# Sample states read and updated through four tiles of the array side by side, heads h and h+2 paired in partition halves

## The reference

```python
# q, logf, k: (B, L, H, 128); v: (B, L, H, 128); s0: (B, H, 128, 128); per block of tokens:
A = jnp.cumsum(lfc, axis=1)
inter = jnp.einsum('bthk,bhkv->bthv', qc * jnp.exp(A), S)
...
scores = jnp.einsum('bthk,bshk,btshk->bths', qc, kc, decay)
intra = jnp.einsum('bths,bshv->bthv', scores, vc)
AL = A[:, -1]
S_new = (jnp.exp(AL)[..., None] * S
         + jnp.einsum('bshk,bshv->bhkv', kc * jnp.exp(AL[:, None] - A), vc))
...
# then: o = rmsnorm per head * gnorm_w * silu(g); x += concat(conv, o) @ w_out; x += moe(rmsnorm(x))
```

## Time and profile before

| what | value |
|---|---|
| median of 3 runs | 1188.64 us (1186.55 to 1191.05) |
| the profiled execution, its own time | 1185.52 us |
| its span, first to last instruction | 1183.6 us |
| mean granted clock of PE | 0.985 of full speed |
| busy: PE, PEld, DVE, ACT, POOL | 95%, 40%, 35%, 14%, 3% |
| DMA, mean over the span | 365 GB/s |

### The profile page before, as it was taken

The page is one execution under the profiler, slowest core; times in us unless marked ns, Lnnn a source line. Parts: engine busy times, 40 slices in busy tenths (PEclk is TensorE's granted clock), DMA queues, the critical chain, the costliest instruction groups (busy, mean ns, idle before and its releaser), DMA issues.

```text
span 1183.6 us, 14962 instructions
## 1 busy us (share of the span) xinstructions
PE 1125.0 (95%) x5841; PEld 468.7 (40%) x5841; DVE 410.0 (35%) x702; ACT 167.7 (14%) x287; POOL 36.2 (3%) x55
## 2 busy tenths in 40 slices
PE   6999999899999999999999999999999999999994
PEld 5787864433333333333333333333333333333331
DVE  2144184643333333333333333333333333333333
ACT  3100112511111111111111111111111111111112
POOL 0000121110000000000000000000000000000000
PEclk9999999889999999999999999999999999999996
DMA  9962126569999999999999999999999999999991
GB/s 303 334 192 84 72 80 207 190 250 412 428 426 428 430 427 429 428 427 430 427 429 429 427 431 427 427 430 427 427 430 427 427 430 429 427 430 427 427 429 58
DMA packets 47375, 432.05 MB, mean 365 GB/s; under 512 B 3824, under 2 KB 18740, under 8 KB 22774
## 3 DMA queue, kind: packets, MB, share of 16 engines
q1 hardware_dynamic: 45792, 428.14, 87.6%
q0 software_dynamic: 752, 2.77, 0.8%
q10 hardware_dynamic: 805, 0.82, 0.2%
HBM read 428.00 MB, written 3.71 MB: 365 GB/s over the span
## 4 chain that ended last, share of the span: by engine, by line
PE 65%; DMA 30%; ACT 2%; DVE 2%; issue 1%; SPq 0%; ACTq 0%; DVEq 0%
PE ps L1153 36%; DMA ring<-in_w_up 15%; DMA ring<-in_w_gate 14%; PE ps L939 9%; PE ps L1109 4%; PE ps L1136 4%; PE ps L1041 3%; PE ps L1144 2%; PE ps L1192 1%; PE ps L958 1%; PE ps L927 1%; ACT R L521 1%; DMA x<-in_x_sample 1%; PE ps L1022 1%; PE ps L1119 1%
## 5 line engine op out<-in xcount | busy, mean ns | idle before, releaser
L1153 PE MATMUL ps<-ring,R 128*64 128x512 f32 x3072 | 694.1, 596 | 15.4 <-DMA ring<-in_w_up 10.4
L1153 PEld LDWEIGHTS ps<-ring,R 128*64 128x64 f32 x3072 | 210.2, 137 | 415.9 <-issue 368.4
L816 DVE SCALAR_TENSOR_TENSOR x<-ps,gates,x 128x1024 f32<-128x1024 f32 (+1 forms) x96 | 123.0, 1281 | 131.4 <-PE ps L1136 131.4
L939 PE MATMUL ps<-R,ring 128*128 128x320 f32 x384 | 112.1, 443 | 1.2 <-DVE R L579 1.2
L823 DVE TENSOR_TENSOR R<-ps,R 128x512 f32<-128x512 f32 x32 | 22.1, 692 | 240.5 <-ACT R L524 240.5
L850 DVE TENSOR_SCALAR R<-ps 128x512 f32<-128x512 f32 x32 | 22.1, 692 | 184.5 <-PE ps L1153 184.5
L939 PEld LDWEIGHTS ps<-R,ring 128*128 128x128 f32 x384 | 71.7, 193 | 29.4 <-issue 2.7
L1136 PE MATMUL ps<-R 64*128 64x512 bf16 (+1 forms) x576 | 79.3, 381 | 0.0
L1109 PE MATMUL ps<-R,P 128*64 128x512 bf16 (+1 forms) x594 | 74.9, 386 | 1.5 <-DVE P L795 1.5
L517 ACT ACTIVATE R<-R 128x512 f32<-128x512 f32 x32 | 20.2, 632 | 318.3 <-DVE R L848 318.3
L1136 PEld LDWEIGHTS ps<-R 64*128 64x128 bf16 (+1 forms) x576 | 21.5, 98 | 88.9 <-issue 51.9
(11 more groups left out here) (198 smaller groups left out, 598.1 us busy)
## 6 DMA issues: line engine op xcount, KB each, us to landing
ring<-in_w_gate SPq DMA_DIRECT2D x64, 2048.0 KB, 29.6
ring<-in_w_up SPq DMA_DIRECT2D x64, 2048.0 KB, 31.5
ring<-in_w_down SPq DMA_DIRECT2D x64, 2048.0 KB, 32.4
ring<-in_w_in SPq DMA_DIRECT2D x14, 1024.0 KB, 12.0
ring<-in_w_out SPq DMA_DIRECT2D x4, 1024.0 KB, 10.1
new_hgrn_sample<-ring POOLq DMA_DIRECT2D x1, 2048.0 KB, 10.9
x<-in_x_prompt SPq DMA_DIRECT2D x2, 512.0 KB, 6.0
y_prompt<-R SPq DMA_DIRECT2D x2, 512.0 KB, 2.6
```

Source lines behind the costliest of these rows:

```text
L816: STT(x[0:n, b, :], ps[0:n, 6:8, :].rearrange("p a n -> p (a n)"), gates[0:n, par, b:b + 1], x[0:n, b, :], ALU.mult, ALU.add).then_inc(acc ...
L939: ins = MM(ps[:, n % 2, 0:NT], slot_k(L, 256)[:, k, 128 * half:128 * half + 128], hT[:, k, :], start=(k == 0), stop=(k == KT - 1))
L1153: ins = MM(ps[64 * half:64 * half + 64, bank, :], lhs(k), w[:, 512 * half:512 * half + 512], start=False, stop=(k == KT - 1))
```

## The change

The heads of a pair are now h and h+2 instead of 2p and 2p+1, and their sample tiles lie in the two partition halves of one bank instead of in two banks (`lev`, `ktok`, the values and the scores). A step `s0q` (p) is put behind unit g1 and behind unit g2: for each of the pair's heads and each half of the samples, 32 queries are the stationary operand and four states (512 columns) the moving one, four such products to a pair, each to its own 32 PSUM partitions. Each gives every query against four states; DVE picks the right one by four masked operations of 128x128. In `o` one product against a piece of the identity adds the outcome in place of the 8 products by sample. `sts` is done by pair: four products with 32 contraction rows each, from four row groups, into four banks. POOL scales all states as soon as `s0q` has read them and makes `vSel`, half as large, behind the last `o`. The second `s0q` and the first move the later steps two places back in the list; `sts` takes two places instead of four.

```diff
@@ -50,7 +50,8 @@
...
     STEPS = ([("lev", l, p) for l in range(NLEV + 1) for p in range(2)] + [("cross",)] + [("o", h) for h in range(NH)]
-             + [("ss", h) for h in range(NH)] + [("ktok",), ("pause",), ("stp",)] + [("sts", h) for h in range(NH)])
+             + [("ss", h) for h in range(NH)] + [("ktok",), ("pause",), ("stp",)] + [("sts", p) for p in range(2)])
+    STEPS[10:10] = [("s0q", p) for p in range(2)]
...
@@ -94,13 +95,14 @@
...
         kS = view(R1, 3840, "p (h t) -> p h t", shape=(4, NT), h=4)
-        vSel = [view(R1, at, "p (b d) -> p b d", shape=(8, 128), b=8) for at in (2560, 3584)]
+        vSel = [view(R1, at, "p (b d) -> p b d", shape=(4, 128), b=4) for at in (2560, 3072)]
...
         q = view(R2, 1280, "p (h t) -> p h t", shape=(4, NT), h=4)
+        s0qS = view(R2, 1280, "p (a d) -> p a d", shape=(2, 128), a=2)
...
@@ -130,6 +132,8 @@
...
         levMask = sb("levMask", [128, NLEV, 128], u8)
+        identS = sc[:, 2, 384:448]
+        levMaskS = sc[:, 3, 384:432].bitcast(u8).rearrange("p (l t) -> p l t", l=3)
...
@@ -221,6 +226,10 @@
...
         START = 1
+
+        def bank(h):
+
+            return 2 + 2 * (h % 2) + h // 2
...
@@ -317,18 +326,15 @@
...
             pool.dma_start(rb[:], A["router_b"][0].partition_broadcast(128)).then_inc(routerIn, 16)
+            pool.wait_ge(s0qMM, 2)
+            pool.wait_ge(f8Out, 1)
             for h in range(NH):
-                if h == 0:
-                    pool.wait_ge(oMM, NH)
-                    pool.wait_ge(f8Out, 1)
-                if h == 1:
-                    pool.wait_ge(kTokMM, 1)
-                if h >= 2:
-                    pool.wait_ge(stSMM, h - 1)
-                pool.tensor_tensor(vSel[h % 2][0:64], v[0:64, 2, 128 * h:128 * h + 128].unsqueeze(1).broadcast_to([64, 8, 128]),
-                                   seqMask[0:64, :].unsqueeze(2).broadcast_to([64, 8, 128]), ALU.mult).then_inc(vSelDone, 1)
...
                                    ALU.mult).then_inc(s0Scaled, 1)
+            pool.wait_ge(oMM, NH)
+            for p in range(2):
+                pool.tensor_tensor(vSel[p], v[:, 2, 128 * p:128 * p + 128].unsqueeze(1).broadcast_to([128, 4, 128]),
+                                   seqMask[:, 0:4].unsqueeze(2).broadcast_to([128, 4, 128]), ALU.mult).then_inc(vSelDone, 1)
...
@@ -408,8 +414,7 @@
...
                     else:
-                        act.activation(v[0:64, 2, 0:256], ps[0:64, n % 2, 0:256], ACT.Copy)
-                        act.activation(v[0:64, 2, 256:512], ps[64:128, n % 2, 0:256], ACT.Copy).then_inc(out, 1)
+                        act.activation(v[:, 2, 0:256], ps[:, n % 2, 0:256], ACT.Copy).then_inc(out, 1)
...
@@ -431,10 +436,10 @@
...
                                    ACT.Copy)
-                    act.activation(kTok[0:64, 8:12, :].rearrange("p n d -> p (n d)"), ps[0:64, 2, :], ACT.Copy).then_inc(kTokOut, 1)
+                    act.activation(kTok[:, 8:10, :].rearrange("p n d -> p (n d)"), ps[:, 2, 0:256], ACT.Copy).then_inc(kTokOut, 1)
...
                     act.wait_ge(stPMM, 1)
-                    act.activation(stP.rearrange("p h d -> p (h d)"), ps[:, 3, :], ACT.Copy).then_inc(stPOut, 1)
+                    act.activation(stP.rearrange("p h d -> p (h d)"), ps[:, 6, :], ACT.Copy).then_inc(stPOut, 1)
...
@@ -590,11 +595,14 @@
...
             dve.wait_ge(maskInSem, 16)
+            did(dve.tensor_copy(levMaskS[0:64], maskIn[0:64, 0:3, 0:64]))
+            did(dve.tensor_copy(levMaskS[64:128], maskIn[64:128, 0:3, 64:128]))
+            did(TT(identS, ident[:, 0:64], ident[:, 64:128], ALU.add))
...
-            pairs = lambda ap, p: ap[:, 2 * p:2 * p + 2, :]
+            pairs = lambda ap, p: ap[:, p:NH:2, :]
...
@@ -641,14 +649,14 @@
...
                     tiles = pb[:, :, 0:256].rearrange("p h (b t) -> p h b t", b=2)
-                    smp = pb[0:64, :, 256:320]
+                    smp = ps[:, 2 + 2 * p, 256:320]
                     outT = pairs(sc, p)[:, :, 0:256].rearrange("p h (b t) -> p h b t", b=2)
-                    outS = pairs(sc, p)[0:64, :, 384:448]
+                    outS = sc[:, p, 384:448]
...
                         did(TT(outT, tiles, ident.unsqueeze(1).unsqueeze(1).broadcast_to([128, 2, 2, 128]), ALU.mult))
-                        need(did(TT(outS, smp, ident[0:64, 0:64].unsqueeze(1).broadcast_to([64, 2, 64]), ALU.mult)))
-                        mq = [UIDX[("q", 2 * p)], UIDX[("q", 2 * p + 1)]]
-                        need(kDone[2 * p + 1])
+                        need(did(TT(outS, smp, identS, ALU.mult)))
+                        mq = [UIDX[("q", p)], UIDX[("q", p + 2)]]
+                        need(kDone[p + 2])
...
@@ -659,8 +667,7 @@
...
                         if l <= 3:
-                            m_ = later_blocks(levMask[0:64, l - 1, 0:64], l)
-                            m_ = m_.unsqueeze(1).broadcast_to([64, 2] + list(m_.shape[1:]))
+                            m_ = later_blocks(levMaskS[:, l - 1, :], l)
...
@@ -679,13 +686,22 @@
...
                     need(did(TT(g[:, h, :], g[:, h, :], sc[:, h, 0:NT], ALU.mult)))
-                    TT(mixT[:, NH + h, :], ps[:, 2 + h, 0:NT], g[:, h, :], ALU.mult).then_inc(mixDone, 1)
+                    TT(mixT[:, NH + h, :], ps[:, bank(h), 0:NT], g[:, h, :], ALU.mult).then_inc(mixDone, 1)
+                elif kind == "s0q":
+                    p = item[1]
+                    dve.wait_ge(s0qMM, p + 1)
+                    part_ = lambda j: ps[:, 6 + p, 128 * j:128 * j + 128]
+                    need(did(TS(s0qS[:, p, :], part_(0), seqMask[:, 0:1], None, ALU.mult)))
+                    for j in (1, 2):
+                        need(did(STT(s0qS[:, p, :], part_(j), seqMask[:, j:j + 1], s0qS[:, p, :], ALU.mult, ALU.add)))
+                    did(STT(s0qS[:, p, :], part_(3), seqMask[:, 3:4], s0qS[:, p, :], ALU.mult, ALU.add), s0qOut)
                 elif kind == "sts":
-                    h = item[1]
-                    dve.wait_ge(stSMM, h + 1)
-                    dve.wait_ge(s0Scaled, h + 1)
-                    TT(s0v[:, :, h, :], s0v[:, :, h, :], ps[:, 4:6, :].rearrange("p a (b d) -> p (a b) d", d=128), ALU.add)\
-                        .then_inc(stSOut, 1)
+                    p = item[1]
+                    dve.wait_ge(stSMM, p + 1)
+                    dve.wait_ge(s0Scaled, NH)
+                    for half, h in enumerate((p, p + 2)):
+                        TT(s0v[:, :, h, :], s0v[:, :, h, :],
+                           ps[:, 2 + 2 * half:4 + 2 * half, :].rearrange("p a (b d) -> p (a b) d", d=128), ALU.add).then_inc(stSOut, 1)
...
@@ -934,31 +949,29 @@
...
                         for k in range(KT):
-                            if beside:
-                                beside(k)
...
                                      start=(k == 0), stop=(k == KT - 1))
-                        beside = None
...
                         for kk in ("f", "q"):
-                            for h in (2 * p, 2 * p + 1):
+                            for h in (p, p + 2):
...
                                 pe.wait_ge(unitOut[m % 2], m // 2 + 1)
-                        pe.wait_ge(kScaled, 2 * p + 2)
+                        pe.wait_ge(kScaled, p + 3)
...
                     cols = (lambda ap: ap) if l == 0 else lambda ap: later_blocks(ap, l)
-                    for hh in range(2):
-                        h = 2 * p + hh
+                    for h in (p, p + 2):
                         for b in range(2):
-                            ins = MM(cols(ps[:, 2 + h, 128 * b:128 * b + 128]), kS[:, h, 128 * b:128 * b + 128],
+                            ins = MM(cols(ps[:, bank(h), 128 * b:128 * b + 128]), kS[:, h, 128 * b:128 * b + 128],
                                      cols(src[:, h, 128 * b:128 * b + 128]), start=True, stop=True)
-                        if l <= 3:
-                            ins = MM(cols(ps[0:64, 2 + h, NP:NT]), kS[:, h, NP:NT], cols(src[:, h, NP:NT]), start=True, stop=True)
+                    if l <= 3:
+                        for half, h in enumerate((p, p + 2)):
+                            ins = MM(cols(ps[64 * half:64 * half + 64, 2 + 2 * p, NP:NT]), kS[:, h, NP:NT], cols(src[:, h, NP:NT]),
+                                     start=True, stop=True)
...
@@ -967,27 +980,30 @@
...
                     h = item[1]
+                    half, p = divmod(h, 2)
...
                         pe.wait_ge(crossOut, 1)
-                        pe.wait_ge(s0In, 16)
-                    o = ps[:, 2 + h, :]
+                        pe.wait_ge(s0qOut, 2)
+                    o = ps[:, bank(h), :]
                     hv = slice(128 * h, 128 * h + 128)
+                    rows = slice(64 * half, 64 * half + 64)
...
                     MM(o[:, 128:256], v[:, 1, hv], sc[:, h, 128:256], start=False, stop=False, skip_group_check=True)
-                    MM(o[:, NP:NT], v[0:64, 2, hv], sc[0:64, h, 384:448], start=False, stop=False, skip_group_check=True)
-
```

(58 more changed lines are left out.)

2 lines of the change are left out of this document (1 added, 1 removed).

## The result

The changed kernel takes 1177.01 us (median of 4 runs, 1176.75 to 1178.02), the kernel before beside it 1189.85 (1186.55 to 1194.48); the ratio is 0.9887 with the 95% interval 0.9855 to 0.992. The forecast was 1178.1 us, range 1175.0 to 1184.5. The two profiled executions are closer to each other, 1185.52 and 1177.10, and why the medians are further apart is the main thing that the experiments looked for.

A forecast was written before the change was run, and what follows sets the result against it. PE's front was taken to set the experts' start and so the end. Removing 16.6 us, adding new steps and waits and shortening levels gave -10.5 us: 1188.6 to 1178.1 us, range 1175.0 to 1184.5.

The forecast's parts named there:

- What bounds the kernel: Whole kernel: the end lies a fixed stretch behind the first up-weights issue, which hangs on PE's front; experts unchanged.
- two s0q steps: New steps reading the old states, four products beside each other: 1.1 us each, 2.2 us added; bounds 1.0 and 3.5 a step.
- two sts steps: State update by pair from four row groups: 1.2 us each, 2.4 us added; bounds 1.0 and 3.7.
- eight levels with sample tiles: Levels with both sample tiles behind the large products, fewer shape changes: 1.5 us less, bounds 0 and 2.6.
- wait of the first level: Ahead of the first level: PE waits for ACT's copy of q2, the unit just ahead; 0.7 us added.
- wait of ktok: Ahead of ktok: PE stands for ACT's root after ss3, now directly ahead; about 0.85 us added.
- the 16.6 us that went: PE time removed: 7.5 us for 32 products by sample in the heads, 9.1 us for state updates and their stand.
- Carrying the difference to the median: Profiled execution took 1185.5 us, 3.1 below the runs' median; that difference carried over, so 1188.6 was the start.
- Two beside each other: Rival in s0q and sts: only two tiles run together, 2.0 us a step, 1181.5 us; chance 0.17.
- one after another, and emptying the array at each tile: Rival in s0q and sts: 16 products run singly, 1.05 us each, 16.8 in place of 4.6, 1190.3 us; chance 0.06.
- DVE was not late at the list's end: Rival at the list's end: two units wait 2 us each for banks DVE has not emptied, 1182.1 us; chance 0.10.
- Nor did the gain fail to arrive: Rival at the experts' start: it hangs on a transfer, so time stays at 1186 to 1189 us; chance 0.07.

The follow-up runs named there:

- e3: Changed kernel with the four side by side products of each s0q step issued four times instead of once; 1179.85 us.
- e11: Changed kernel with a unit put ahead of cross and of ktok, and q units ordered q0, q2, q1, q3; 1171.31 us.
- e12: Changed kernel run and profiled again, no edit; 1176.01 us, ratio 0.9891 to the kernel before.
- e2: Changed kernel with one unit between last level and cross tile, and one between last sum of squares and ktok; 1172.63 us.
- e5: Kernel before, profiled once more, no edit; 1195.69 us.
- e6: Kernel before, profiled another time, no edit; 1191.24 us.
- e9: Kernel before with each of the 32 products by sample taking 64 columns instead of 8, into a spare bank part; 1186.39 us, ratio 0.9972.
- e8: Changed kernel with the update in two row groups of 64 instead of four of 32; 1178.06 us.
- e10: Changed kernel without s0q steps, its 8 products by sample per head restored but with 64 columns instead of 8; 1178.35 us.

## Why the prediction was right

The forecast missed the median by 1.1 us, and the mechanism is the one that it named: PE's front gets shorter by tiles that run four at a time, and the end follows it. But that it came so close is partly luck. In the sum a term that was too small and one that was missing nearly cancelled each other, and two errors in the step from the profiled execution to the median did so as well.

**What bounds the kernel** held without a change: the experts' length from the first up issue is the same within 1.8 us in all profiles, and e3 shows the front passing on its length. The prediction read DMA's share of the front, 0.27, from one stretch; in the kernel before it is 0.69 from 49 to 95 us and 0.21 from 95 to 189, so the reading stands where the change works.

**The terms.** Read in the first two profiles, the projection starts 10.39 us earlier; the sum said 10.5.

| term | forecast | measured |
|---|---|---|
| two s0q steps | +2.2 | +1.98 |
| two sts steps | +2.4 | +2.14 |
| a head's extra product, four times (1.35 us from 141.85 to 143.20, against 1.12) | +1.0 | +0.9 |
| eight levels with sample tiles (1.53 to 1.17) | -1.5 | -2.9 |
| ktok's products in place of transpositions | +0.4 | +0.3 |
| wait of the first level (the stand; 0.9 by e11 and e12) | +0.7 | +0.7 |
| wait of ktok (157.84 to 159.16, a product of 0.54) | +0.8 | +0.8 |
| wait of cross (121.00 to 123.59, a level of 0.84) | none | +1.75 |

The levels were mis-sized: I let a quarter to a half of the extra 0.66 us go and took a little over a quarter. Two sample tiles beside each other now cost 0.33 us together (1.17 less 0.84), what one had cost. That is past my bound of 2.6 us for eight. (The lower end of the range is off as well: with the levels at that bound and no stands the terms give 1175.4 us, not 1175.0.) The wait of cross is the failing of the search for new waits: level 7 of the second pair and cross came to stand side by side in the list, as `ss3` and `ktok` did, and I followed only the latter. e2 shows both on the path. With the 16.6 us that went these make 10.9; 0.5 us is not assigned.

**Carrying the difference to the median** was the weak step. I took the profiled execution as a fair sample and added the 3.1 us by which it lay below the runs. It lay below because it was spared the clock falls that e5 and e6 show. Three things came of it.

First, its own execution gained 8.4 us, not 10.5, and the first up issue came at 240.73 us, not 239.1. From the projection to the first product of expert 0 the changed kernel needs 57.10 us (178.01 to 235.11) where the kernel before needs 56.04 (188.40 to 244.44), with the clock at 0.50 sooner in the router's sparse stretch, and about 1 us more goes in the first expert and after.

Second, the medians gained more than the profiles: 12.8, 16.6 and 14.5 us in three sets, where 10.5 were forecast. Some 4 us are the heads' clock (e9). The falls by the update cost 1.6 to 3.2 us in three of four profiles that have its stand, and the changed kernel has neither stand nor fall there; what they cost in the median was not tried by itself. From e9 to e12, in one set, 10.4 us are left.

Third, the starting point was low: 1188.6 us from 3 runs, where 45 later ones have the median 1190.2. The changed kernel's 16 runs have 1176.5. So the gain was forecast 3.2 us too small and the start 1.6 too low. The two errors go against each other, and with all these runs the miss is 1.6 us.

**The rivals.** Two beside each other, one after another, and emptying the array at each tile fell by e3 and e8 and by the 0.99 and 1.07 us. By the figure of the Trainium skill ("TensorE: Matmul & The Clock Gate", Part 3, 3.07 times for four row tiles) `sts` would have taken 1.15 us, an estimate; it took 1.07 (3.3 times), and the four column tiles, repeated, 0.89 us in place of 3.5, which is 3.9 times. DVE was not late at the list's end: no stand is left between `ss3` and the projection but the one for ACT. Nor did the gain fail to arrive, by e3.

## What to carry to other kernels

When steps are moved in an order written out by hand, list every pair of dependent steps that have become neighbours, and put an independent block of work back between them; here that was worth 2.7 us between the first level and the projection, a quarter of what the change itself gained there. Four float32 products side by side, with 32 rows or 32 columns each, cost little more than one full product (1.07 and 0.99 us a set, 0.89 repeated, against 0.88); pairs with 64 rows or 64 columns cost about one too. And profile the kernel before more than once before a small difference is forecast: one execution can hide a clock state that others of the same program have.

## What was not expected of the hardware

The granted clock fell to 0.50 while PE was busy in every moment, with 4 of 5 us of weight loading, behind and among products of 8 columns; with 64 columns in the same places it stayed at 1.00 in the heads (e9, e10, one profile each). In two of three profiles of the kernel before, these falls cost 8.3 and 5.0 us, and falls by the update another 3.2 in each; the third profile had none (stretch between 150.35, 147.07 and 138.88). A fall can also follow a short stand, and need not: behind the stand of 1.4 us in the update it came in three of four profiles (e5, e6, e9), behind the one of 1.6 us ahead of the cross tile in one of seven (e8).
